# How the old cache rows are laid on the partitions, and which queue loads the value cache, in a decoder step with dilated attention

## The reference, cut to what matters

```
BRANCHES = ((128, 1), (512, 4), (2048, 16))
for w, d in BRANCHES:
    nj = w // d
    j = jnp.arange(nj + 1)
    idx = n_past + jnp.arange(n_new)[:, None] - j[None, :] * d
    kg, vg = kc[:, jnp.maximum(idx, 0)], vc[:, jnp.maximum(idx, 0)]
    logits = einsum('bthe,btjhe->bhtj', q, kg) * scale + bias
    p, s, lse = softmax_stats(logits, valid)
    o = einsum('bhtj,btjhe->bthe', p, vg) / s
```

## Time and profile before

| | before |
|---|---|
| median of three runs | 1722.02 us |
| the profiled execution's own time | 1721.44 us |
| its span, first to last instruction | 1719.7 us |
| PE busy | 1578.1 us (92% of the span) |
| DVE, ACT busy | 500.2 us (29%), 245.8 us (14%) |
| queue of SP (q1) | 488.31 MB, 75.3% of 16 DMA engines |
| queue of ACT (q10) | 27.53 MB, 5.7% of 16 DMA engines |
| HBM traffic | 304 GB/s over the span |

### The profile page before, as it was taken

How to read it: one execution, slowest core, us unless ns; L and a number is a source line. 1 busy time by engine, 2 the same in 40 slices (tenths; PEclk the granted TensorE clock), 3 DMA queues, 4 the chain that set the end, 5 groups by cost and what they waited for, 6 DMA issues and landing times.

```text
span 1719.7 us, 22183 instructions
## 1 busy us (share of the span) xinstructions
PE 1578.1 (92%) x7660; PEld 641.3 (37%) x7661; DVE 500.2 (29%) x1115; ACT 245.8 (14%) x445; POOL 14.4 (1%) x24
## 2 busy tenths in 40 slices
PE   5999897877766999999999999999999999999994
PEld 1655655544433233333333333333333333333331
DVE  2110443323345212322323222223223223222235
ACT  0000422222011101111111110111111111111110
POOL 0000100000000000000000000000000000000000
PEclk9999778998877899999999999999999999999997
DMA  9859528999592577999999986999999999976950
GB/s 337 312 234 287 173 98 251 284 277 277 151 281 101 199 270 273 355 387 408 402 382 416 400 318 236 346 375 408 393 404 395 398 402 390 404 295 240 342 244 31
DMA packets 104019, 523.45 MB, mean 304 GB/s; under 512 B 10316, under 2 KB 10629, under 8 KB 65882
## 3 DMA queue, kind: packets, MB, share of 16 engines
q1 hardware_dynamic: 94954, 488.31, 75.3%
q10 hardware_dynamic: 7056, 27.53, 5.7%
q0 software_dynamic: 1984, 7.26, 1.5%
HBM read 519.60 MB, written 3.46 MB: 304 GB/s over the span
## 4 chain that ended last, share of the span: by engine, by line
PE 82%; DMA 9%; DVE 5%; issue 1%; ACTq 1%; SPq 1%; ACT 0%; POOL 0%; DVEq 0%; POOLq 0%
PE ps L1441 30%; PE ps L1495 15%; PE ps L1072 7%; PE ps L1384 6%; PE ps L1368 6%; DMA arena<-in_cache_v 5%; PE ps L1136 5%; PE ps L1425 4%; PE ps L1297 3%; PE ps L1133 2%; DMA arena<-in_w_in 2%; DMA arena<-in_ln_b 2%; ACTq L556 1%; PE ps L1317 1%; PE ps L1248 1%
## 5 line engine op out<-in xcount | busy, mean ns | idle before, releaser
L1441 PE MATMUL ps<-arena 128*64 128x512 f32 x2240 | 510.9, 616 | 0.0
L1441 PEld LDWEIGHTS ps<-arena 128*64 128x64 f32 x2240 | 162.9, 142 | 348.1 <-issue 348.1
L1495 PE MATMUL ps<-arena 128*64 128x512 f32 x1120 | 254.4, 598 | 3.2 <-DVE arena L1001 1.4
L1072 PE MATMUL ps<-arena 128*128 128x128 f32 (+4 forms) x1170 | 180.8, 294 | 68.7 <-DVE arena L766 13.1
L1072 PEld LDWEIGHTS ps<-arena 128*128 128x128 f32 (+4 forms) x1170 | 134.5, 149 | 156.0 <-issue 86.0
L1019 DVE TENSOR_SCALAR arena<-ps 128x512 f32<-128x512 f32 x35 | 24.2, 691 | 539.0 <-PE ps L1441 539.0
L1495 PEld LDWEIGHTS ps<-arena 128*64 128x64 f32 x1120 | 75.3, 136 | 176.4 <-issue 176.4
L979 DVE TENSOR_TENSOR arena<-arena,ps 128x512 f32<-128x512 f32 (+1 forms) x198 | 124.0, 678 | 55.8 <-PE ps L1384 44.4
L1384 PE MATMUL ps<-arena 64*128 64x512 f32 x444 | 122.1, 635 | 0.0
L1368 PE MATMUL ps<-arena 128*64 128x512 f32 (+1 forms) x444 | 108.9, 610 | 2.4 <-DVE arena L967 2.4
L628 ACT ACTIVATE arena<-arena 128x512 f32<-128x512 f32 x35 | 22.1, 630 | 522.4 <-DVE arena L1019 522.4
(11 more groups left out here) (212 smaller groups left out, 852.3 us busy)
## 6 DMA issues: line engine op xcount, KB each, us to landing
arena<-in_w_up SPq DMA_DIRECT2D x256, 1024.0 KB, 8.8
arena<-in_w_down SPq DMA_DIRECT2D x128, 1024.0 KB, 7.2
arena<-in_w_ada SPq DMA_DIRECT2D x12, 2048.0 KB, 14.7
arena<-in_cache_k SPq DMA_DIRECT2D x48, 384.0 KB, 7.7
arena<-in_cache_v ACTq DMA_DIRECT2D x42, 384.0 KB, 12.2
arena<-in_w_in SPq DMA_DIRECT2D x6, 2048.0 KB, 19.9
arena<-in_cache_k SPq DMA_DIRECT2D x8, 1536.0 KB, 11.4
arena<-in_cache_v ACTq DMA_DIRECT2D x7, 1536.0 KB, 7.6
```

The lines of the kernel that those rows point to most:

```text
L1072: return nc.tensor.transpose(o, i, ident[0:n, 0:n])
L1441: ins = mm(bank(2 * v + part)[64 * h:64 * h + 64], xe_t[:, v, at:at + 64], up_w[:, k, FF * part + 512 * h:FF * part + 512 * h + 512], star ...
L1495: ins = mm(bank(3 - v)[64 * h:64 * h + 64], lhs, dn_w[:, kk, 512 * h:512 * h + 512], start=kk == 0, stop=kk == KC - 1)
```

## The change

The old rows get the partition order of the bias tables, the permuting copy becomes one plain copy, and the loads of the values go from ACT's queue to SP's.

```diff
             def load_old(cache, sb, b, done):
-                old = cache[b][:, 0:PAST - REC, :].rearrange("o (r g i) d -> r (o g) i d", r=6, g=16)
-                for r in range(6):
-                    sp.dma_start(sb[:, 4 + r, :], old[r, :, 0:8]).then_inc(done, 16)
+                old = cache[b][:, 0:PAST - REC, :].rearrange("o (r g i) d -> i (o g) r d", r=6, g=16)
+                for i in range(8):
+                    sp.dma_start(sb[16 * i:16 * i + 16, 4:KB, :], old[i]).then_inc(done, 16)
...
+            def load_values(b, used):
+                sp.wait_ge(v_used, used)
+                load_rec(cv, v_sb, b, v_in)
+                load_old(cv, v_sb, b, v_in)
...
             with sp.Fori(1, NB - 1) as b:
                 load_keys(ck[1:NB], bass.ds(b, 1), b)
-
+                load_values(bass.ds(b, 1), b)
+            load_values(slice(NB - 1, NB), NB - 1)
...
             act_norm(0)
-            act_batch(0, True)
-            with act.Fori(1, NB - 1) as b:
-                load_values(bass.ds(b, 1), b)
+            with act.Fori(0, NB - 1) as b:
                 act_batch(b, True)
-            load_values(slice(NB - 1, NB), NB - 1)
             act_batch(NB - 1, False)
...
-            v_.tensor_copy(s_bias[0:96, 0:REC], ps[0:96, 0:REC])
-            v_.tensor_copy(s_bias[0:96, NCACHE:SB], ps[0:96, NCACHE:SB])
-            V(v_.tensor_copy(s_bias[0:96, REC:NCACHE].rearrange("q (r g i) -> q r i g", r=6, g=16),
-                             ps[0:96, REC:NCACHE].rearrange("q (r i g) -> q r i g", r=6, i=8)))
+            V(v_.tensor_copy(s_bias[0:96, :], ps[0:96, 0:SB]))
...
-                    pe.wait_ge(k_old_in, b * 96 + 96)
+                    pe.wait_ge(k_old_in, b * 128 + 128)
...
-                pe.wait_ge(v_in, b * 112 + 112)
+                pe.wait_ge(v_in, b * 144 + 144)
```

More of the change, by code:

```diff
@@ L547, in act_norm @@
                 nc.scalar.activation(norm_rep[g], norm_rep[g], ACT.Sqrt).then_inc(sd_ready, 1)
[L550 to L556, removed]
             def act_batch(b, more):
```

## The result

The changed kernel takes 1837.63 us (median of four runs, 1824.39 to 1844.76) against 1721.73 us before; 23 executions of it are on record, from 1809.93 to 1846.74 us. The two medians give a ratio of 1.067; leaving out the executions more than 1.5% above a kernel's fastest, as every ratio with an interval here does, it is 1.061 (1.056 to 1.066). Slower by 6 to 7%, as forecast; 1862 us was the forecast, 1775 to 1900 the range.

The account below looks back on a forecast made before the run. Sample attention was taken as bound by its cache loads, though most of the kernel is expert matmuls. 1721.4 us plus 141 us for slower loads and 0 for the rest gave 1862 us, range 1775 to 1900.

Parts of the forecast that it names:

- Part 1: Old rows' new layout: DMAs into 16 neighbouring partitions slow the loads to 113 GB/s, between 101 and 125.
- T: Time of one load of old rows: 9.5 us before, forecast 20.9 us after.
- a halving times 1.22: Old layout's rate read as 404 GB/s halved to 202, with a factor 1.22 won back by engines drifting.
- Part 2: Keys and values on SP's one queue: transfers lie end to end, the loop's loads take 329 us, 141 us more.
- 13 T + 57: Length in us of the stretch from second batch's old keys to last values: 13 old loads, 12 recent, 9 us extra.
- Part 3: Early loads of batches 0 and 1 and the bias tables: all hidden, ending by 226 us, cost 0.
- Parts 4 and 5: One bias copy of 1.6 us, gain hidden; ACT's table loads of 1.28 us a turn, hidden: both 0.
- A: Rival: old rows' rate falls less, to 125 to 220 GB/s; at 163, +57 us, 1779 us; chance 0.19.
- B: Rival: source, not destination, sets 250 GB/s, so not slower: 1714 us, or 1693 at 300 GB/s; chance 0.12.
- C: Rival: narrow DMAs disturb each other, below 99 GB/s, 1900 us and over; chance 0.05.
- D: Rival: SP's single queue holds keys back while DMA engines idle, 36 us, 1757 us; chance 0.04.
- The signs: Expected profile of the batch loop: DMA share near 1.0, mean 158 GB/s, PE waits about 10 us, landings up to 20.

Follow-up runs that it names:

- one_stride: Kernel before, value loads moved to SP's queue, each old-row DMA reading 128 single rows at one stride (other cache rows than asked for): 1684.16 us.
- groups_act: Kernel before with the cache as 128 groups of 16 rows, three DMAs a load instead of seven, one bias copy, values on ACT's queue: 1679.78 us, ratio 0.979.
- layout_only: Changed kernel with the value loads of batches 1 to 7 back on ACT's queue: 1837.82 us, ratio 1.070.

## Why the prediction was right, point by point

- **The bound.** Right: the sample attention is bound by its loads at the rate of the old rows. With the loads at full rate (`one_stride`, `groups_act`) the kernel falls to 1684 and 1680 us and PE's 21.9 us a batch remains.
- **Part 1, the rate.** The mechanism held: same sources elsewhere, 207; other sources, same destinations, 123. The size was off. 113 GB/s was taken, 122 to 126 measured where old rows run alone, so T was 18.7 to 19.3 us instead of 20.9. That lies at the upper end given (125). The 113 came out of reading 247 as "a halving times 1.22"; the ratio 122 / 247 is one more halving of the whole, factor included. I had taken the middle between with and without. The stated assignment, 16 engines with eight neighbours each, isn't shown by any row. `one_stride` shows that another order of the source removes the loss; the third DMA of `groups_act`, for which the same theory gave 250 and which ran at 400, leaves open what sets the 250 GB/s of the layout before.
- **Part 2, end to end.** The formula 13 T + 57 with T = 19.3 gives 308, and 308.2 were measured. The mean of 168 GB/s from 264.39 to 533 us bears it out: an old and a recent load in 19.3 + 4.0 us would be 169. The match to 0.2 us is partly luck, since for today's layout the same formula is 8 us short. The 1.5, 1.4 and 1 us of start and landing in it had no row behind them. The queue was priced at nothing; alone, on the layout of before, it costs 18 us (1.05%), and in the profile the last values are there at 464.33 instead of 454.87. On the new layout no cost is seen: the medians of four runs are 1837.63 us with one queue and 1837.82 with two (`layout_only`), and the ratios, 1.061 (1.056 to 1.066) and 1.070 (1.065 to 1.075), don't stand the other way. Forecast error of the sum: 141 - 120 = 21 us, of which 13 x 1.6 = 21 is the rate.
- **Part 3, early loads.** Right: they end at about 218 us, before 226, and PE's first scores start at 247.56 (247.74 before).
- **Parts 4 and 5.** Right: 1.61 us for the copy, behind it the same wait for PE; seven table loads of 1.28 us, and each runs while ACT waits.
- **Rivals.** A (125 to 220 GB/s) holds at its very edge: the last load alone runs at 128. B and C are excluded by the rates, D by `layout_only`, but its doubt about the single queue had a small truth in it, of another kind: lower throughput, no keys held back.
- **The signs.** The waits of about 10 us each for old keys and for values were 6.8 and 13.0 on the mean, the clock falls to 0.50 in them, and the mean rate is 161 GB/s where 158 was given. One sign was too low: an old row's DMA lands 24.0 us after its issue in the median and 38.3 at most, where up to 20 was given.

## What to carry to other kernels

A DMA share near 1.0 says nothing about the rate; read the GB/s beside it, in a stretch where one kind of load is alone, against the best the same kernel shows elsewhere. A load whose DMAs write into few neighbouring partitions at a time can pay by halves: 396, 207 to 250, 122 GB/s for the same bytes in the same pieces. Before choosing a partition order, look for one outer stride over all 128 partitions on the DRAM side, even across a border that the computation draws, as between old and recent rows here, and measure the rate of each shape alone: several shapes here did not run as the theory said.

## What the runs showed of the hardware that was not expected

- 96 partitions at one outer stride, with a quarter of the bytes on 32 others: 225 GB/s, and 237 while the first 96-partition DMA is alone, where 128 at one stride gave 396. How the 96 are dealt to the engines was not seen.
- 32 groups of four partitions in 6 KB pieces ran at 400 GB/s or more, where 16 groups of eight in 3 KB pieces run at 243 to 251.
- The narrow DMAs carry 122 to 128 GB/s whenever they are alone, at 153 and at 553 us; whether they speed up in between, where the stretch from 454 to 466 shows 138, can't be told apart from recent rows among them.
- Two queues carry 280 GB/s where one carries 267, at a DMA share near 1.0 both times. In the 96-partition layout the kernel with two queues is 17 us faster.
